# Prompt attention of a hybrid decoder trunk: the scores of a pair of heads issued together, masks after both, and the two maxima one behind the other

## The reference, cut to what matters

```
def _attend(q, k, v, mask):
    s = jnp.einsum('btkgd,bskd->bkgts', q, k) * SCALE
    p = _masked_softmax(s, mask)
    return jnp.einsum('bkgts,bskd->btkgd', p.astype(v.dtype), v)
```

## Time and profile before

| | |
|---|---|
| median of 3 runs | 2859.05 us (2856.82 to 2872.66) |
| profiled execution, its own time | 2861.02 us |
| its span in the trace | 2859.5 us |
| PE busy | 2657.9 us (93%) |
| DVE busy | 1022.5 us (36%) |
| ACT busy | 719.9 us (25%) |
| POOL busy | 343.4 us (12%) |
| mean granted TensorE clock | 0.929 of full speed |
| prompt attention, layer 0 | 716.28 to 902.37 us |
| prompt attention, layer 1 | 2126 to 2310.94 us |

### The profile page before, as it was taken

One profiled execution on the slowest core, in us unless ns is written; L12 is line 12 of the kernel. 1 busy time (PEld: TensorE's weight loads), 2 busy tenths in 40 slices (PEclk: granted clock), 3 DMA queues, 4 the chain that ended last, 5 costly groups with the idle time before them and its releaser, 6 DMA issues.

```text
span 2859.5 us, 49629 instructions
## 1 busy us (share of the span) xinstructions
PE 2657.9 (93%) x18108; PEld 2377.1 (83%) x18108; DVE 1022.5 (36%) x1877; ACT 719.9 (25%) x1132; POOL 343.4 (12%) x321
## 2 busy tenths in 40 slices
PE   8999999998898899999899999999978888999996
PEld 8999788896456899999899997888944567999995
DVE  2222111535453642232442211224456437222416
ACT  3221000422342332231232210014223423222313
POOL 0000000023132200013100000001151311000230
PEclk9999899997876899999999999999968859999998
DMA  4222443113422212222222234321153302222222
GB/s 148 89 88 85 151 135 107 59 61 124 138 78 71 74 60 89 88 85 81 85 74 89 88 112 151 127 92 61 42 178 112 87 33 74 83 84 85 89 86 91
DMA packets 110163, 267.13 MB, mean 93 GB/s; under 512 B 15364, under 2 KB 85155, under 8 KB 90787
## 3 DMA queue, kind: packets, MB, share of 16 engines
q1 hardware_dynamic: 99922, 234.26, 24.2%
q0 software_dynamic: 10080, 30.73, 3.4%
HBM read 259.20 MB, written 14.24 MB: 96 GB/s over the span
## 4 chain that ended last, share of the span: by engine, by line
PE 51%; issue 36%; POOL 3%; DVE 3%; SPq 2%; DMA 1%; ACT 1%; POOLq 1%; DVEq 1%; PEldq 0%; PEld 0%; ACTq 0%
PE PS L485 50%; POOL wo_lo L416 2%; SPq L334 1%; POOL wi_lo L474 1%; DVEq L1469 1%; DMA M<-slc_k_dram 1%; DMA WO<-wo_dram 1%; PE PS L979 1%; POOLq L425 1%; DVE xs L1594 0%; DVE sm L1942 0%; POOLq L429 0%; ACT WO L1145 0%; DVE WO L1472 0%; SPq L330 0%
## 5 line engine op out<-in xcount | busy, mean ns | idle before, releaser
L485 PE MATMUL PS<-xs,wi_hi 128*128 128x272 f32 x5376 | 1012.1, 288 | 4.9 <-DVE wi_lo L1472 2.5
L485 PE MATMUL PS<-xs,wi_lo 128*128 128x272 f32 x2960 | 859.2, 290 | 0.0
L485 PEld LDWEIGHTS PS<-xs,wi_hi 128*128 128x128 f32 x5376 | 843.8, 188 | 5.5 <-issue 5.5
L485 PEld LDWEIGHTS PS<-xs,wi_lo 128*128 128x128 f32 x2960 | 562.6, 190 | 0.0
L416 POOL TENSOR_TENSOR wo_lo<-WO,wo_hi 128x2816 fp32r<-128x2816 f32 x24 | 150.7, 6280 | 1892.6 <-ACT wo_hi L1145 1892.6
L485 PE MATMUL PS<-H,WO 128*128 128x272 f32 x1408 | 331.8, 397 | 6.5 <-DMA WO<-wo_dram 5.0
L1472 DVE TENSOR_TENSOR wi_lo<-WI,wi_hi 128x2048 fp32r<-128x2048 f32 x81 | 185.6, 2292 | 415.0 <-ACT wi_hi L1145 415.0
L485 PEld LDWEIGHTS PS<-H,WO 128*128 128x128 f32 x1408 | 268.8, 192 | 67.4 <-issue 12.2
L485 PE MATMUL PS<-wo_hi,xs 128*128 128x352 f32 x960 | 239.8, 328 | 14.6 <-DVE xs L1594 8.2
L1145 ACT ACTIVATE wi_hi<-WI 128x2048 fp32r<-128x2048 f32 x81 | 155.1, 1915 | 332.8 <-DMA WI<-wi_dram 332.8
L485 PE MATMUL PS<-h_hi,wo_hi 128*128 128x272 f32 x704 | 207.5, 295 | 26.0 <-POOL wo_lo L416 16.6
(11 more groups left out here) (205 smaller groups left out, 3055.8 us busy)
## 6 DMA issues: line engine op xcount, KB each, us to landing
WI<-wi_dram SPq DMA_DIRECT2D x96, 1024.0 KB, 4.9
WO<-wo_dram SPq DMA_DIRECT2D x44, 1408.0 KB, 6.0
M<-cmp_t_dram SPq DMA_DIRECT2D x256, 128.0 KB, 2.3
M<-slc_k_dram SPq DMA_DIRECT2D x128, 64.0 KB, 2.2
M<-slc_k_dram POOLq DMA_DIRECT2D x128, 64.0 KB, 2.4
M<-slc_v_dram SPq DMA_DIRECT2D x128, 64.0 KB, 2.2
M<-slc_v_dram POOLq DMA_DIRECT2D x128, 64.0 KB, 2.3
o_win_s_dram<-win_rows_dram POOLq DMA_DIRECT2D x2, 4064.0 KB, 4.0
```

The lines of the kernel that those rows point to most:

```text
L485: return nc.tensor.matmul(out, lhsT, rhs, start=start, stop=stop, skip_group_check=True)
```

## The change

`scores` takes a pair instead of a unit. It waits once, for the exponential of unit 2w - 1, issues the 64-row product of head 0 on rows 0 to 63 and that of head 1 on rows 64 to 127, and then both masks. The loop calls it at even u. On DVE, `maxima(u)` and `maxima(u + 1)` follow each other at even u. ACT's order, the banks and the pieces' indices are as before.

```
-                def scores(u):
-                    t, g, br, kv = unit(u)
+                def scores(w):
+
+                    t, g, br, _ = unit(2 * w)
                     n = (t + 1) * P
-                    if u >= 2:
-                        pe.wait_ge(p_ready, at(l, 64, u - 1))
-                    r = slice(kv * HD, kv * HD + HD)
-                    mm(PS[:, u % 2, 0:n], qT[r, g, t * P:(t + 1) * P], kT[r, br, 0:n], True, False)
-
-                    mm(PS[:, u % 2, n - P:n], TRI[:, 1, :], TRI[:, 0, :], False, True).then_inc(sc_ready, 1)
+                    if w >= 1:
+                        pe.wait_ge(p_ready, at(l, 64, 2 * w))
+                    for kv in range(2):
+                        r = slice(kv * HD, kv * HD + HD)
+                        mm(PS[:, kv, 0:n], qT[r, g, t * P:(t + 1) * P], kT[r, br, 0:n], True, False)
+                    for kv in range(2):
+
+                        mm(PS[:, kv, n - P:n], TRI[:, 1, :], TRI[:, 0, :], False, True).then_inc(sc_ready, 1)
...
-                    if u < 64:
-                        scores(u)
+                    if u < 64 and u % 2 == 0:
+                        scores(u // 2)
...
-                    if u < 64:
+                    if u < 64 and u % 2 == 0:
                         maxima(u)
+                        maxima(u + 1)
```

## The result

With the change the kernel took **2832.77 us** (median of 4 runs, 2826.83 to 2834.87). The kernel before, run beside it, took 2861.11 (4 runs). The ratio is 0.9902, 95% interval 0.9878 to 0.9925: 28 us or 1.0% faster. A later measurement of the same kernel gave 2829.81 against 2858.05, ratio 0.9907 (0.9891 to 0.9922). The forecast was 13.5 us and a range down to 2835; the sign was right, the size half of what came.

What follows compares the result with a forecast made beforehand. PE, busy 93% of the span, was taken as the bound except where key transfers, DVE or POOL's list fix an end. Gains of 7.2 + 5.5 + 0.8 = 13.5 us gave 2846 us, 80% range 2835 to 2866.

Steps and rivals of the forecast that it cites:

- The rival with three passes: A pair's scores take about 1.6 us, or the ring is longer; about 4 us of gain left, 2855; 20%.
- stretch 2: From `keys_2` to `win_values`, 83.28 us in layer 0, 79.57 in layer 1; forecast gain 7.2 and 5.5 us.
- stretch 3: From `win_values` to `slc_values` 3: as long as POOL's list of page loads, up to 4.15 us less; gain nothing.
- ahead of the DVE windows: Layer 0, 740 to 752, full clock: 2.5 pairs with PE pieces to fill their slack, gain 1.5 us.
- in the DVE windows I count nothing: Three windows in stretch 2, 38.2 us, DVE busy 33.6: no gain counted, DVE's idle 4.6 us the most possible.
- the factor 32/45: Half-clock time of stretch 2, layer 1 over layer 0; scales layer 0's 5.7 us of half-clock gain for layer 1.
- a rival with 10%: Pairs inside DVE's windows use its idle 4.6 us and POOL's pause goes: another 4 to 5 us a layer, 2837.
- stretch 4: From `slc_values` 3 to the end of attention, four pairs of tile 0: gain taken as 0.4 us a layer.
- the ring: Pair's scores wait for the previous exponential: 4.25 us pair to pair at tile 3, full clock; 0.95 us becomes a wait.
- stretch 1: From the attention stage's start to `keys_2`, its end set by the transfer of keys; gain nothing.
- PE's busy time: Over the whole kernel it should fall by some 30 us, more than twice what the span falls.
- The rival in which it falls in stretch 3 (13%): Clock falls to half as PE idles; 8 us over in each layer, kernel slower at 2871; 13%.

Runs made afterwards that it cites:

- e1: The change, but head 0's mask stands between the two 64-row products, so they do not overlap; 2852.75 us, ratio 0.9982 to the kernel before.
- e3: The change with pairs issued together only in units 0 to 27, single units elsewhere; 2834.19 us, ratio 0.9909 to the kernel before.
- e5: The change with pairs issued together only in units 28 to 55, single units elsewhere; 2855.47 us, ratio 0.999 to the kernel before.
- e2: The change on PE alone, with DVE's maxima in their old order; 2834.68 us, ratio 0.9916 to the kernel before.
- e4: The change with pairs issued together only in units 56 to 63, single units elsewhere; 2853.05 us, ratio 0.9984 to the kernel before.
- e7: The change, with both exponentials of a pair ahead of the copy on ACT; 2831.87 us, ratio 0.99 to the kernel before.
- e10: The change itself, unaltered, measured and profiled a second time; 2829.81 us, ratio 0.9907 to the kernel before.
- e6: The kernel before with DVE's part alone: both maxima at even u, PE issuing scores unit by unit; 3017.61 us, ratio 1.0572.

## Why the prediction was half right

**Right: the mechanism and the place.** The overlap is complete, 1.06 us for what would have been 2.10, and without it 5 of the 28 us are left (`e1`). I had argued it from column groups. The rival with three passes (1.6 us) is out, and with it the strict reading, pass by pass, of the rule of the Trainium skill, "TensorE: Matmul & The Clock Gate", Part 3, that matmuls on different row groups start and end in program order. Two of the pair's four passes are at work from 734.02 on, and the mask stands after two pass times. The rows don't tell which pass is whose, so the rule taken product by product is neither shown nor refuted here.

**Right: stretch 2 carries the gain, stretch 3 gives most of its own back.** `e3` and `e5` show both. The part "ahead of the DVE windows" was sized at 1.5 us and is 1.7 in layer 1 (from `keys_2` to the row `PS<-Z,WI 128*64` 16.4 us before, 14.7 after).

**Wrong: "in the DVE windows I count nothing."** In layer 1 the part from `win_scores` to `win_values` went from 35.8 us to 31.6, 4.2 less, and I had counted 2.1 for it in layer 0, which is 1.5 in layer 1 by the factor 32/45. I had taken DVE as the bound in there and its idle time as out of reach. It was partly reachable: DVE idled 2.8 us in the two 8 us windows from 2196 before, and 1.1 us in those from 2172 after. It took both parts of the change: with PE's alone this part stays near 36 us (`e2`), with the orders and no overlap it is 34.5 (`e1`). A likely reading is that the pair's scores are both there, and both maxima ahead of the piece, when DVE enters a long one; no run separates the pieces. This is the term that was short by some 2 to 3 us a layer: the sum counted PE's saved products alone and put the new order at nothing. I had it as a rival with 10%.

**Wrong: stretch 4, "I take 0.4 a layer."** It measured 3.0 (`e4`: 5 us for both layers). I had set one score per pair as the upper bound and then chosen near the middle of a loss and a gain that nothing supported. Rows of before would have told: at half clock, tile 0, a pair was 2.94 us with PE hardly idle, and the scores' second 0.72 us of it could overlap. The first pair lost 0.44, the first three together 1.83 (10.06 to 8.23 us), and the last of the eight units' scores come sooner as well: from the last pair's start to the end 5.76 us (2270.95 to 2276.71) instead of 6.83 (2304.11 to 2310.94). In `e1`, with the orders alone, stretch 4 is 19.2 us: of the 3.0 us, 1.3 are the order's and 1.7 the overlap's.

**Wrong: stretch 3, "nothing."** 2.3 us a layer. The stretch was indeed as long as POOL's list, as predicted, but its start hangs on how quickly `win_values` runs, and that depends on the clock that stretch 2 leaves (3.2 or 5.5 us). I had treated the end of one stretch as if it didn't reach into the next. I had also misread the list: from 826.24 on POOL starts six groups of eight loads, not four, and a pause of about 3 us stands between any two of them, so only about 1.1 of the 4.15 us could go. PE's wait for cached values grew from 5 to 9 and 10 us a layer and not towards 13; a part of PE's saving stands in the waits for DVE's weights instead.

**Wrong, with little harm: the ring.** I had it run through ACT and end in front of the scores with 0.95 us, and wrote that `turn` coming one maximum later "is inside the ring's slack". Most of the slack is used up there instead: the odd `turn` waits 0.56 us for DVE (37.7 us in the whole kernel), against 6.0 us in front of the scores. From the start of the scores to the end of the odd `turn` at tile 3 the pair takes 3.91 us (734.02 to 737.93, the start of the next piece), so 0.44 of the 1.05 us are kept where I had left 0.10, because a piece of PE stands behind it. In stretch 1, where PE has no piece behind a pair and ACT has one in it, the pair is not 4.25 us but 5.78 (719.36 to 725.14); the wait for keys took that up. With DVE's old order the wait is where I had put it (`e2`, 44.4 us). `e7` shows that shortening ACT's part alone moves nothing.

**Wrong: PE's busy time.** I wrote 30 us, it was 60.5. The sum is plain and I had not made it: eight pairs of each tile save one product of 1.05, about 0.84, 0.63 and 0.42 us at full clock, 23.5 us a layer, 47 for both, more at half clock.

**The clock.** The rival in which it falls in stretch 3 (13%) didn't come. From 812 to 847 the window of the change has PE busy 29.77 of 35 us, and the clock is full:

```profile
812.00:847.00 35.00, 29.77 (x352) 19.18 (x350) 18.64 (x66) 21.07 (x71) 16.80 (x31) 1.00 0.43 121
848.00:852.00 4.00, 3.76 (x67) 3.24 (x66) 0.00 (x0) 0.00 (x0) 1.99 (x4) 0.57 0.35 98
```

It falls in the second row, behind a wait of 1.97 us for cached values. The mean clock of the whole stretch is 0.88 and 0.91 with the change (0.92 and 0.85 in `e10`) against 0.93 and 0.92 before. But the mechanism exists in this kernel: `e6` comes close to that rival, with waits of 1.48 us in the pairs of tile 3; its stretch 3 of layer 0 has a mean clock of 0.66 and takes 96.5 us.

What stays open: how much of the gain in stretch 2 is time in which PE's rows themselves ran at a higher clock, and how much is work taken out. The mean clock of its windows was 0.73 and 0.80 before and 0.81 to 0.82 after, but `e4` has 0.82 there with the old code and 78.3 us, so I ascribe the larger part to the work; this was not separated. The same holds for the split between overlap and order: `e1` takes the overlap away and keeps the order, but its stretch 1 also ran at a lower clock (0.65 against 0.75).

## What to carry to other kernels

In this kernel two 64-row products of different heads that stand next to each other in the program take the time of one, float32 in two passes too; a single 128-row instruction between them ends that. When the bound engine is made faster, split its stage at the points that something else fixes (a transfer, a list of loads, the end), and size each piece by what fixes its end, including the last one, which has nothing behind it to wait for. Count what the new order does for the engine that is handed the work, and not only what the bound engine saves. Where two engines hand units to each other in an order written by hand, change both orders together: PE's half of this change is worth 24 us, DVE's half alone costs 160.

## What the runs showed of the hardware that was not expected

Both passes of both heads overlap completely: 1.06 us for 4 x 512 columns against 1.05 for 2 x 512, at half clock 2.50 against 2.94 us for a whole pair of tile 0. With 90.9 us of waits for DVE's weights on PE, 1.48 us each in the pairs of tile 3, the mean granted clock over the whole kernel was 0.894 instead of 0.929, and the same instructions kept PE busy for 88.9 us more (`e6`). With waits of about 0.55 us once a pair it was 1.00 (812 to 847 us of the change). POOL's pause between two groups of eight loads is at least 2.87 us in every kept trace, also between the two groups of one half, where the program has no wait (3.01 us at 835.24 before).
